# One decode-step kernel: the value loads of the paged attention move from GpSimd's queue to SyncE's, in one order with the key loads

## The chip, the cores and the metric

The kernel runs on one core of a Trainium2 chip. Its time is in device microseconds (us), the median of three runs. Engines have the profile's short names: PE is TensorE, DVE VectorE, ACT ScalarE, POOL GpSimd, SP SyncE. SP computes nothing here; it only issues DMAs and waits on semaphores.

## The reference, cut to what matters

One layer of a hybrid decoder, for a prompt of 256 tokens and for 8 decode batches of 4 tokens each. The stage that matters here is the decode attention, batch by batch:

```
k_all = concatenate([cache_fox_k[page_table], fk])       # 8 pages x 128 tokens, 6 heads x 128, then 4 new tokens
v_all = concatenate([cache_fox_v[page_table], fv])       # the same for the values
s = q k^T * HEAD_DIM**-0.5 + (c_q - c_k)                 # c: cumulative log-forget
fox_o = softmax(where(k_pos <= q_pos, s, -inf)) v_all
mem_o = softmax(q mk^T * HEAD_DIM**-0.5) mv              # 256 memory tokens, 4 heads x 128, own cache for each batch
```

Which pages a batch has stands in `page_table`, an input (8 pages for each of 8 batches), so the address of each page is read at run time. A page of keys or of values is 128 tokens x 768 floats, 393,216 bytes. The memory keys or values of a batch are 256 tokens x 512 floats, 524,288 bytes. After the attention come the output projection, a router and 32 experts, whose weights (three matrices of 2048 x 512 each) are read in whole.

## The kernel before, in words

Each engine has its own program, and semaphores set the order between them. The stages run one after another: norms and the input projection (up to some 450 us), the recurrence, head norms and outputs by token (to about 600 us), the attention of the prompt (to 655 us), the decode attention (655 to 819 us), the output projection (to about 970 us), the router and the experts.

**PE in the decode attention.** For each batch, `key_in(b, i)` transposes the keys in 14 units: units 0 to 11 read the eight key pages, two pages by three units, and units 12 and 13 the memory keys. Each unit waits for the pages that it reads (`k_in`, `mk_loaded`) and counts `kt_filled` when it is done, which frees pages. `decode_scores(b)` makes the scores, `max_row`, `max_spread` and `probs_in` stand between later key units, and `decode_values(b)` multiplies the probabilities by the value pages. It waits for the batch's eight value pages (`v_in`), for its memory values (`mv_loaded`), and at its end it counts `d_pv`. `decode_heads(b)` closes the batch. The order on PE is: keys of batch b + 1, values of b, scores of b + 1, heads of b, keys of b + 2, and so on.

**Buffers.** There is one set of eight key pages (`kpage`), reused by each batch as PE frees them, two sets of eight value pages (`vpage[par]`, par is the batch's parity), one buffer of memory keys (`mk_in`) and one of memory values (`mv_in`).

**Who loads what.** SP issues the key pages and the memory keys (lines 552 to 572). `load_key_page` first reads the page number from `ptab_row` in SBUF into a register (`value_load`, line 553), then waits for `kt_filled` (line 555), then issues the DMA (line 556). Six of batch 0's pages go ahead of the wait for the end of the prompt's attention (`pa_out`), since their buffers are free sooner. The loop over the other batches follows, then the first output-weight slice (line 576).

POOL issues the value pages and the memory values (lines 755 to 774): batch 0's pages as soon as it has finished its part of the recurrence and the projection is done, batch 0's memory values after `pa_out`, batch 1's pages after the outputs by token have been written, and then, for each batch, when `d_pv` says that the values of the batch before are used:

```
pool.wait_ge(d_pv, i * 2 + (u + 1))
load_mem_values(i * 2 + (u + 1))
load_values(i * 2 + (u + 2), u)
```

The two engines' DMAs go through two queues (in the profile q1, hardware_dynamic, for SP and q0, software_dynamic, for POOL) to the same 16 DMA engines. Nothing but the semaphores above orders the one queue against the other. After its last load POOL waits for the output projection and clears a strip of 32 rows.

Of the kernel before, what the change touches and what calls it, by code (L numbers as in the profile page):

```python
# [7 lines left out]
P = 128  # L8
KC = D // P
SEQ = 256  # L10
NB, NL = 8, 4
# [4 lines left out]
HF, HG, HM = 6, 6, 4  # L16
# [3 lines left out]
NPG, PG = 8, 128  # L20
POOL = 80
# [23 lines left out]
def build(nc, x_prompt, x_sample, cache_fox_k, cache_fox_v, cache_fox_logf, cache_mem_k, cache_mem_v,  # L45
# [7 lines left out]
    ds = bass.ds  # L53
# [16 lines left out]
    v_pages = cache_fox_v[0].rearrange("g t h d -> g t (h d)")  # L70

    ctx = ExitStack()
    with ctx:
        ctx.enter_context(nc.allow_non_contiguous_dma(reason="small vectors and column blocks"))

        def sb(name, shape, dt=f32):
            return ctx.enter_context(nc.sbuf_tensor(name, shape, dt))

        def sem(name):
            return ctx.enter_context(nc.semaphore(name))  # L80
# [30 lines left out]
        def view(off, *dims):  # L111
            n = 1
            for d in dims:
                n *= d
            a = arena[:, off:off + n]
            if len(dims) == 2:
                return a.rearrange("p (a b) -> p a b", b=dims[1])
            if len(dims) == 3:
                return a.rearrange("p (a b c) -> p a b c", b=dims[1], c=dims[2])
            return a  # L120
# [24 lines left out]
        def heads2(n):  # L145
# [22 lines left out]
        vpage = [[view(WORK + (4 + g) * FW, FW) for g in range(NPG)],  # L168
                 [view(MTOK + 5 * MEM + g * FW, FW) for g in range(6)] + [view(RAW + FV * T + g * FW, FW) for g in range(2)]]
# [4 lines left out]
        mv_in = view(MRAW + 2 * MW, 2, MW)  # L174
# [97 lines left out]
        ptab_row = sb("ptab_row", [1, NB * NPG], i32)  # L272
# [35 lines left out]
        blk_filled = sem("blk_filled")  # L308
# [23 lines left out]
        out_done = sem("out_done")  # L332
# [26 lines left out]
        h_again = sem("h_again")  # L359
# [21 lines left out]
        yt_filled = sem("yt_filled")  # L381
# [15 lines left out]
        s_loaded = [sem(f"s_loaded{n}") for n in range(2)]  # L397
# [18 lines left out]
        pa_out = sem("pa_out")  # L416
        ptrow_in = sem("ptrow_in")
# [3 lines left out]
        v_loaded = sem("v_loaded")  # L421
# [3 lines left out]
        q_clear = sem("q_clear")  # L425
        q_set = sem("q_set")
        d_scored = sem("d_scored")
        v_in, V_IN0 = (v_loaded, s_loaded[0]), (0, 16 * HG // 2)
        mv_loaded, MV0 = s_loaded[1], 16 * HG // 2
        d_row, d_row_min, d_spread = lb_diff, lb_exp, ssq_clear  # L430
        d_max = sem("d_max")
        d_exp = sem("d_exp")
# [5 lines left out]
        d_pv = sem("d_pv")  # L438
# [49 lines left out]
        NU = len(UNITS)  # L488
# [12 lines left out]
        def _(sp):  # L501
# [50 lines left out]
            def load_key_page(b, g, first=False):  # L552
                page = sp.value_load(ptab_row[0:1, ds(b * NPG + g, 1)], min_val=0, max_val=POOL - 1)
                if not first:
                    sp.wait_ge(kt_filled, b * KU + (3 * (g // 2) + 3 - KU))
                sp.dma_start(kpage[g], k_pages[ds(page, 1)].rearrange("g t n -> t (g n)")).then_inc(k_in[g], 16)

            def load_mem_keys(b, first=False):
                if not first:
                    sp.wait_ge(kt_filled, b * KU)  # L560
                sp.dma_start(mk_in, cache_mem_k[0][ds(b, 1)].rearrange("b (a t) h d -> t (b a) (h d)", t=P)).then_inc(mk_loaded, 16)
# [4 lines left out]
            for g in (3, 4):  # L566
                load_key_page(0, g, True)
            load_mem_keys(0, True)
            with sp.Fori(0, NB - 1) as i:
                for g in range(NPG):  # L570
                    load_key_page(i + 1, g)
                load_mem_keys(i + 1)


            sp.wait_ge(hn_done, NN)
# [91 lines left out]
        def _(pool):  # L667
# [80 lines left out]
            for n in range(2):  # L748
                pool.wait_ge(sts_out[n], 16 * HG // 2)


            pool.wait_ge(ptrow_in, 16)
            pool.wait_ge(blk_filled, 55)

            def load_values(b, par):
                for g in range(NPG):
                    page = pool.value_load(ptab_row[0:1, ds(b * NPG + g, 1)], min_val=0, max_val=POOL - 1)
                    pool.dma_start(vpage[par][g], v_pages[ds(page, 1)].rearrange("g t n -> t (g n)")).then_inc(v_in[par], 16)

            def load_mem_values(b):  # L760
                pool.dma_start(mv_in, cache_mem_v[0][ds(b, 1)].rearrange("b (a t) h d -> t (b a) (h d)", t=P)).then_inc(mv_loaded, 16)

            load_values(0, 0)
            pool.wait_ge(pa_out, NU)
            load_mem_values(0)
            pool.wait_ge(out_done, 16 * N_ROWS_OUT)
            load_values(1, 1)
            with pool.Fori(0, (NB - 2) // 2) as i:
                for u in range(2):
                    pool.wait_ge(d_pv, i * 2 + (u + 1))  # L770
                    load_mem_values(i * 2 + (u + 1))
                    load_values(i * 2 + (u + 2), u)
            pool.wait_ge(d_pv, NB - 1)
            load_mem_values(NB - 1)

            pool.wait_ge(wo_drained, KC)
            pool.memset(h_scaled[:, 2, :], 0.0).then_inc(consts_set, 1)
# [1311 lines left out]
N_ROWS_OUT = 8  # L2089
# [28 lines left out]
```

## Time and profile before

| | us |
|---|---|
| median of 3 runs (1952.29, 1952.88, 1958.1) | 1952.88 |
| the profiled execution | 1950.19 |
| its span, first to last instruction | 1948.6 |
| PE busy | 1571.3 (81%) |
| DVE busy | 435.0 (22%) |
| ACT busy | 223.2 (11%) |
| POOL busy | 77.4 (4%) |
| mean granted clock of PE | 0.881 |

How to read it: busy times are sums over the span, and matmuls are pipelined, so that a busy PE isn't PE at its peak. The granted clock is a share of 2.4 GHz: 1.00 is 2.4 GHz and 0.50 is 1.2 GHz. The waiting of SP and its DMA issues are in no engine's busy time; they are seen in the timeline of SP's queue, which the profile calls SPq (and POOL's POOLq).

### The profile page before, as it was taken

How to read it: one execution, taken by the hardware profiler on the slowest of the kernel's cores; microseconds unless marked ns; L12 is line 12 of the kernel's file. 1: busy time of each engine (PE TensorE's matmuls, PEld its weight loads, DVE VectorE, ACT ScalarE, POOL GpSimd, SP SyncE). 2: the span in 40 equal slices, each digit the busy share in tenths (PEclk: the TensorE clock that was granted, in tenths of full speed). 3: DMA queues.
4: the chain of work that ended last, by engine and by line, in shares of the span. 5: the costliest groups of instructions: out<-in, count | busy, mean ns of one | idle time of the engine just before them, and what ended most of it. 6: DMA issues, size and time to landing. Idle time of an engine off the chain costs nothing.

```text
span 1948.6 us, 24082 instructions
## 1 busy us (share of the span) xinstructions
PE 1571.3 (81%) x9517; PEld 925.7 (48%) x9517; DVE 435.0 (22%) x1138; ACT 223.2 (11%) x502; POOL 77.4 (4%) x141
## 2 busy tenths in 40 slices
PE   5999999999989899999967658677585766857656
PEld 4777777777746667677643213132141312313111
DVE  2200066645332434211220201102020020200201
ACT  3000101110042323111220000000000000000000
POOL 1000000012100122100000000000000000000000
PEclk9999999999986899899978888887788887878877
DMA  7434423234204599665369999999999999999996
GB/s 227 129 131 142 147 99 113 81 129 125 79 1 172 198 368 399 233 194 184 138 263 421 421 421 421 422 422 422 422 422 422 422 422 422 422 422 422 421 421 253
DMA packets 140424, 555.05 MB, mean 285 GB/s; under 512 B 16611, under 2 KB 71972, under 8 KB 90084
## 3 DMA queue, kind: packets, MB, share of 16 engines
q1 hardware_dynamic: 132084, 517.83, 67.0%
q0 software_dynamic: 8272, 36.25, 5.2%
q8 instruction: 50, 0.82, 0.2%
q14 instruction: 18, 0.15, 0.0%
HBM read 545.32 MB, written 8.72 MB: 284 GB/s over the span
## 4 chain that ended last, share of the span: by engine, by line
PE 57%; DMA 33%; DVE 3%; SPq 2%; ACT 2%; issue 2%; POOL 0%; DVEq 0%; ACTq 0%
PE PS L1544 19%; DMA arena<-in_w_up_e_dram 18%; DMA arena<-in_w_down_e_dram 9%; PE PS L1985 7%; PE PS L1932 7%; PE PS L2017 4%; DMA arena<-in_w_gate_e_dram 3%; PE PS L1964 3%; PE PS L2032 3%; PE PS L1804 2%; SPq L598 2%; DMA arena<-in_cache_mem_k_dram 2%; PE PS L1585 1%; PE PS L1864 1%; PE PS L1821 1%
## 5 line engine op out<-in xcount | busy, mean ns | idle before, releaser
L1985 PE MATMUL PS<-arena 128*32 128x512 f32 x2048 | 323.5, 779 | 225.6 <-DMA arena<-in_w_up_e_dram 148.1
L1544 PE MATMUL PS<-arena 128*128 128x288 f32 (+1 forms) x1728 | 434.2, 407 | 3.4 <-DVE arena L1036 1.1
L1544 PEld LDWEIGHTS PS<-arena 128*128 128x128 f32 x1728 | 328.4, 192 | 95.1 <-issue 12.9
L1985 PEld LDWEIGHTS PS<-arena 128*32 128x32 f32 x2048 | 78.6, 137 | 461.6 <-issue 188.6
L2017 PE MATMUL PS<-arena 128*32 128x512 f32 x1024 | 157.3, 776 | 73.6 <-DMA arena<-in_w_down_e_dram 73.6
L1932 PE MATMUL PS<-arena 128*128 128x288 f32 x512 | 129.5, 412 | 0.4 <-DVE arena L1308 0.4
L2017 PEld LDWEIGHTS PS<-arena 128*32 128x32 f32 x1024 | 37.8, 138 | 186.0 <-issue 98.0
L1461 DVE TENSOR_TENSOR arena<-arena,PS 128x512 f32<-128x512 f32 x8 | 5.5, 688 | 518.9 <-PE PS L1985 518.9
L1932 PEld LDWEIGHTS PS<-arena 128*128 128x128 f32 x512 | 97.2, 192 | 31.6 <-issue 5.5
L1964 PEld LDWEIGHTS PS<-arena 128*128 128x128 f32 x768 | 89.3, 196 | 9.7 <-issue 7.5
L1964 PE MATMUL PS<-arena 128*128 128x128 f32 x768 | 91.8, 281 | 2.0 <-ACT arena L965 2.0
L2032 PE MATMUL PS<-arena 128*128 128x512 f32 (+1 forms) x192 | 85.5, 598 | 0.0
L1471 DVE TENSOR_TENSOR arena<-arena,PS 128x512 f32<-128x512 f32 (+1 forms) x96 | 65.6, 684 | 18.8 <-PE PS L2032 18.8
L1804 PE MATMUL PS<-ident,arena 128*128 128x128 f32 x448 | 59.0, 288 | 9.1 <-DMA arena<-in_cache_fox_k_dram 5.4
L1466 DVE COPY arena<-PS 128x512 f32<-128x512 f32 x16 | 11.1, 692 | 221.1 <-PE PS L2017 221.1
L1804 PEld LDWEIGHTS PS<-ident,arena 128*128 128x128 f32 x448 | 53.4, 150 | 11.2 <-DMA arena<-in_cache_fox_k_dram 6.0
L2032 PEld LDWEIGHTS PS<-arena 128*128 128x128 f32 (+1 forms) x192 | 30.1, 163 | 55.7 <-issue 43.0
L980 ACT ACTIVATE arena<-PS 128x512 f32<-128x512 f32 x8 | 4.8, 597 | 372.0 <-PE PS L2004 372.0
L1272 DVE COPY arena<-PS 128x512 f32<-128x512 f32 x56 | 38.1, 688 | 28.7 <-PE PS L1804 28.6
L1107 DVE SCALAR_TENSOR_TENSOR arena<-arena 128x576 f32<-128x576 f32 x3 | 2.3, 759 | 187.2 <-ACT arena L814 187.2
L910 ACT ACTIVATE arena<-PS 128x512 f32<-128x512 f32 x56 | 33.4, 597 | 67.9 <-PE PS L1804 67.1
L1444 DVE TENSOR_TENSOR arena<-PS,g_ffn_r 128x512 f32<-128x512 f32 x32 | 22.1, 691 | 83.0 <-PE PS L1964 83.0
(335 smaller groups left out, 1190.4 us busy)
## 6 DMA issues: line engine op xcount, KB each, us to landing
arena<-in_w_gate_e_dram SPq DMA_DIRECT2D x128, 1024.0 KB, 17.6
arena<-in_w_up_e_dram SPq DMA_DIRECT2D x128, 1024.0 KB, 20.4
arena<-in_w_down_e_dram SPq DMA_DIRECT2D x128, 1024.0 KB, 18.5
arena<-in_w_in_dram SPq DMA_DIRECT2D x14, 3072.0 KB, 10.8
arena<-in_cache_fox_k_dram SPq DMA_DIRECT2D x64, 384.0 KB, 9.3
arena<-in_cache_fox_v_dram POOLq DMA_DIRECT2D x64, 384.0 KB, 7.5
arena<-in_w_out_dram SPq DMA_DIRECT2D x8, 2048.0 KB, 9.1
arena<-in_w_mem_kv_dram SPq DMA_DIRECT2D x2, 3072.0 KB, 17.9
```

Of the source, the lines that this page charges most:

```text
L598: sp.dma_start(unit[slot].rearrange("p (k n) -> p k n", n=src.shape[4]), src[ds(p * XQ + x, 1), g % 4].rearrange("e p k n -> p (e k) n")). ...
L910: act.activation(dst, PS[:, key_bank(b, i), :].rearrange("p (h t) -> p h t", h=dst.shape[1]), ACT.Copy).then_inc(kt_act, 1)
L1272: dve.tensor_copy(dst, PS[:, key_bank(b, i), :].rearrange("p (h t) -> p h t", h=dst.shape[1])).then_inc(kt_dve, 1)
L1444: dve.tensor_tensor(xgT[:, 4 * c:4 * c + 4, :], PS[:, 2 + c, :].rearrange("p (c s) -> p c s", s=P), g_ffn_r[:, 4 * c:4 * c + 4].rearrange( ...
L1471: dve.tensor_tensor(o, o, PS[0:w, 2 + n % 4, :], ALU.add).then_inc(part_added, 1)
L1544: last = pe.matmul(PS[0:m, bank, 0:w], wt[:, k, c:c + m], rhs[:, k, :], start=(k == 0), stop=(k == KC - 1))
L1804: last = pe.transpose(PS[:, key_bank(b, i), a * P:(a + 1) * P], src, ident[:, :])
L1932: last = pe.matmul(PS[:, n % 2, 0:T], wo_slot[(n // 2) % 3][:, k, c:c + P], cat[:, k, :], start=(k == 0), stop=(k == KC - 1))
L1964: last = pe.matmul(o, h_scaled[:, t, c * P:(c + 1) * P], pick_tok[:, t, :, :].rearrange("p x s -> p (x s)"), start=(t == 0), stop=(t == 2))
L1985: last = pe.matmul(PS[x * SLOTS:(x + 1) * SLOTS, which, :], xgT[:, kk, x * SLOTS:(x + 1) * SLOTS], wt[:, k, :], start=(kk == 0), stop=(kk ...
L2017: last = pe.matmul(PS[x * SLOTS:(x + 1) * SLOTS, YB[n], :], hT[:, q, x * SLOTS:(x + 1) * SLOTS], wt[:, n * 512:(n + 1) * 512], start=(q == ...
L2032: pe.matmul(PS[0:w, 2 + n % 4, :], gate_slot[:, t0:t0 + w], yslot[:, c * 512:(c + 1) * 512], start=True, stop=True).then_inc(part_filled, 1)
```

## The change: all four kinds of load in SP's program

The loads of values and memory values are taken out of POOL's program and put into SP's. The order on SP is now: key pages 3 and 4 and the memory keys of batch 0, value pages 0, memory values 0, keys 1, value pages 1, and then for each further batch its keys, the memory values of the batch before, and its value pages. The waits are the same (`out_done`, `d_pv`, `kt_filled`), each at the same load as before; the waits for `ptrow_in`, `blk_filled` and `pa_out` need not be repeated, since SP has passed its own. [...] The output-weight slice of line 576 comes after the last memory values.

```
-        v_in, V_IN0 = (v_loaded, s_loaded[0]), (0, 16 * HG // 2)
-        mv_loaded, MV0 = s_loaded[1], 16 * HG // 2
+        v_in, V_IN0 = (v_loaded, h_again), (0, 0)
+        mv_loaded, MV0 = yt_filled, 0
...
             load_mem_keys(0, True)
-            with sp.Fori(0, NB - 1) as i:
+            def load_values(b, par):
                 for g in range(NPG):
-                    load_key_page(i + 1, g)
-                load_mem_keys(i + 1)
+                    page = sp.value_load(ptab_row[0:1, ds(b * NPG + g, 1)], min_val=0, max_val=POOL - 1)
+                    sp.dma_start(vpage[par][g], v_pages[ds(page, 1)].rearrange("g t n -> t (g n)")).then_inc(v_in[par], 16)
+            def load_mem_values(b):
+                sp.dma_start(mv_in, cache_mem_v[0][ds(b, 1)].rearrange("b (a t) h d -> t (b a) (h d)", t=P)).then_inc(mv_loaded, 16)
+            def load_keys(b):
+                for g in range(NPG):
+                    load_key_page(b, g)
+                load_mem_keys(b)
+            load_values(0, 0)
+            load_mem_values(0)
+            sp.wait_ge(out_done, 16 * N_ROWS_OUT)
+            load_keys(1)
+            load_values(1, 1)
+            with sp.Fori(0, (NB - 2) // 2) as i:
+                for u in range(2):
+                    load_keys(i * 2 + (u + 2))
+                    sp.wait_ge(d_pv, i * 2 + (u + 1))
+                    load_mem_values(i * 2 + (u + 1))
+                    load_values(i * 2 + (u + 2), u)
+            sp.wait_ge(d_pv, NB - 1)
+            load_mem_values(NB - 1)
...
-            pool.wait_ge(ptrow_in, 16)
-            pool.wait_ge(blk_filled, 55)
-            def load_values(b, par):
-            ...
-            load_values(0, 0)
-            pool.wait_ge(pa_out, NU)
-            load_mem_values(0)
-            pool.wait_ge(out_done, 16 * N_ROWS_OUT)
-            load_values(1, 1)
-            ...
-            pool.wait_ge(d_pv, NB - 1)
-            load_mem_values(NB - 1)
```

## Rows read from the trace of the kernel before

**Rows 1.** The page's 40 slices of the span: busy tenths of the DMA engines.
```profile
DMA  7434423234204599665369999999999999999996
```

**Rows 2.** Windows: stretch, length, busy PE, PEld, DVE, ACT, POOL; clock, DMA share, GB/s.
```profile
610.00:615.00 5.00, 5.00 (x19) 4.08 (x19) 2.00 (x8) 1.58 (x6) 1.16 (x3) 0.50 1.03 407
...
810.00:815.00 5.00, 5.00 (x38) 1.36 (x32) 0.00 (x0) 0.00 (x0) 0.00 (x0) 0.50 0.00 0
...
656.00:776.00 120.00, 110.40 (x1312) 82.89 (x1311) 49.13 (x130) 40.84 (x84) 29.68 (x54) 0.96 1.00 380
...
1000.00:1940.00 940.00, 640.83 (x3998) 231.88 (x3987) 109.19 (x190) 30.50 (x47) 0.00 (x0) 0.82 1.00 415
```

**Rows 3.** Timeline of POOL: start, length, then the idle time before it and its releaser.
```profile
603.72 0.57 POOL L758 DMA_DIRECT2D arena<-in_cache_fox_v_dram  x1 [89.75 <-issue]
...
687.65 0.71 POOL L761 DMA_DIRECT2D arena<-in_cache_mem_v_dram  x1 [22.46 <-PE PS L1871]
...
705.21 0.71 POOL L761 DMA_DIRECT2D arena<-in_cache_mem_v_dram  x1 [6.23 <-PE PS L1871]
...
798.13 0.71 POOL L761 DMA_DIRECT2D arena<-in_cache_mem_v_dram  x1 [6.85 <-PE PS L1871]
```

**Rows 4.** The chain of waits in order of time, decode attention: start, length, what.
```profile
657.05 6.94 DMA arena<-in_cache_fox_k_dram
...
703.69 15.06 DMA arena<-in_cache_mem_k_dram
...
759.68 15.57 DMA arena<-in_cache_mem_k_dram
```

**Rows 5.** Waits of SP's queue, 650 to 822 us: total, times, longest.
```profile
SPq L556 <- PE PS L1804: 45.5, 8, 9.9
```

**Rows 6.** Timeline of SP's queue: first issue's start, time to the last one's end.
```profile
602.93 6.34 SPq L556 DMA_DIRECT2D arena<-in_cache_fox_k_dram  x6
...
655.95 1.44 SPq L556 DMA_DIRECT2D arena<-in_cache_fox_k_dram  x2
657.42 0.44 SPq L561 DMA_DIRECT2D arena<-in_cache_mem_k_dram  x1
...
694.73 8.78 SPq L556 DMA_DIRECT2D arena<-in_cache_fox_k_dram  x8
703.69 1.16 SPq L561 DMA_DIRECT2D arena<-in_cache_mem_k_dram  x1
...
777.25 0.38 SPq L561 DMA_DIRECT2D arena<-in_cache_mem_k_dram  x1
777.85 0.39 SPq L576 DMA_DIRECT2D arena<-in_w_out_dram  x1
```

**Rows 7.** Lines 553 and 556 on SP: nanoseconds min/median/max, first and last start.
```profile
L553 SPq TENSOR_LOAD <-ptab_row x64: 263/268/459, 602.0 to 776.0; - x64
...
L556 SPq DMA_DIRECT2D arena<-in_cache_fox_k_dram x64: 332/333/379, 602.9 to 776.7; - x64
...
DMA to landing us min/median/max: 3.1/9.3/12.9
```

**Rows 8.** Line 561 on SP, the memory keys, in the same form.
```profile
L561 SPq DMA_DIRECT2D arena<-in_cache_mem_k_dram x8: 383/383/1155, 657.4 to 777.3; - x8
...
DMA to landing us min/median/max: 5.1/13.2/16.4
```

**Rows 9.** Timeline of PE, the end of the stage, in the form of the timelines above.
```profile
775.30 1.09 PE L1804 MATMUL PS<-ident,arena 128*128 128x128 f32 x8 [1.94 <-DMA arena<-in_cache_mem_k_dram]
...
793.89 2.79 PE L1864 MATMUL PS<-arena 128*32 128x512 f32 x32
...
809.30 5.35 PE L1864 MATMUL PS<-arena 128*32 128x512 f32 x32 [0.70 <-DVE arena L1291]
...
819.26 3.12 PE L1932 MATMUL PS<-arena 128*128 128x288 f32 x6 [0.35 <-DVE arena L1308]
```

More of the change, by code:

```diff
@@ L749, in _ @@
                 pool.wait_ge(sts_out[n], 16 * HG // 2)
-            pool.wait_ge(ptrow_in, 16)
-            pool.wait_ge(blk_filled, 55)
-            def load_values(b, par):
[L756 to L761, printed above, removed]
-            load_values(0, 0)
-            pool.wait_ge(pa_out, NU)
-            load_mem_values(0)
-            pool.wait_ge(out_done, 16 * N_ROWS_OUT)
-            load_values(1, 1)
[L768 to L772, printed above, removed]
-            pool.wait_ge(d_pv, NB - 1)
-            load_mem_values(NB - 1)
             pool.wait_ge(wo_drained, KC)
```

## The prediction, made before the change was run

> **What bounds the kernel now.** I read the busy slices first: the DMA engines are at 9 tenths or more from the 22nd slice to all but the last, and before that only in slices 15 and 16, 682 to 779 us [rows 1]. Those two are the decode attention, the only stage that the diff touches. Its windows show three things: from 656 to 776 us TensorE is busy 110.4 of 120 us, the DMA share is 1.00 and 380 GB/s move [rows 2]; so PE and DMA are both close to their limit. Third I read the moments at which POOL issues a memory-value load, since each one marks the end of a batch's value matmuls: 687.65, 705.21 and so on to 798.13, six periods of 18.41 us on average, where an undisturbed one is 17.56 [rows 3]. The missing 0.85 us a batch is DMA: the chain of waits goes through key pages at 657.05 and through memory keys at 703.69 and 759.68 [rows 4]. Last I looked at the engine that is to take the extra work. SP waits 45.5 us in this stage for PE to free key pages, at most 9.9 at a time [rows 5]. That is all the room that it has.
>
> **What the change does, part by part.** Call the eight key pages of a batch K, its memory keys M, its value pages V, its memory values W. Before, SP issues K and M, POOL V and W. After, SP issues everything from one instruction stream, and V0, which POOL issues from 603.72 on [rows 3], comes only after SP's wait for the prompt attention at 655.
>
> *Price of a page.* SP's eight key pages at 694.73 take 8.78 us from the first issue's start to the last one's end [rows 6]. One issue is 0.33 us [rows 7], so they are (8.78 - 0.33)/7 = 1.207 us apart. Nothing holds them there: PE's transposes run well ahead by then, and the six ungated pages at 602.93 are (6.34 - 0.33)/5 = 1.202 apart [rows 6]. The rest of the 1.2 us is a serial chain ahead of each issue, the register load from the page table (268 ns [rows 7]) above all. A value page on SP in the loop has no row: its nearest are these, and the pair at 655.95, 1.44 - 0.33 = 1.11 apart [rows 6]. I take 1.20 for all and keep 1.11 as the low end for those that are not key pages of the loop. M comes 0.51 us after the last key page's issue (703.69 against 703.51 - 0.33), though its own issue once took 1.16 instead of 0.44 [rows 6]; I take 0.52 for each M and W, with 1.16 as the high end.
>
> *The sum on SP.* One batch is now 16 x 1.20 + 2 x 0.52 = 20.2 us of SP, more than the period of 18.41. SP has issued M0 by 657.42 + 0.44 = 657.9 [rows 6]. From there to the issue of M7 stand V0 to V6 and K1 to K7, 112 pages, and W0 to W5 and M1 to M6, 12 loads: 657.9 + 112 x 1.20 + 12 x 0.52 = 798.5. Before, M7 is issued at 777.25 [rows 6]. A second way: added are 56 pages and 6 loads, 70.3 us, of which SP's 45.5 us of waiting pay the larger part, 777.25 + 70.3 - 45.5 = 802; the 3.5 us between the two show how well the sum is known.
>
> *Do the waits on SP hold it up further?* The new wait for the end of the previous batch's values sits between M and W; behind it are queued W, V and the next K. It is passed at once: in this sum SP comes to it some 10 us after PE has passed that point. The same holds for the waits on freed key pages.
>
> *What that does to PE.* PE needs M7 for its last two transposes of batch 7. The landing of M took 5.1 us at least, 13.2 in the median, in the crowded queue [rows 8]. A batch is 16 pages of 393,216 B and two loads of 524,288 B, 7.34 MB. In 20.2 us that is 363 GB/s against the 407 of a full stretch [rows 2]; the queue drains, so I take 5.1: 803.6. The two transposes take 1.09 us and from the start of the value matmuls to POOL's next issue are 798.13 - 793.89 = 4.24 us [rows 3, 9]. So the values of batch 6 end at 808.9, against 798.13: **+10.8 us**. The other batches are late by less, 2 us more with each.
>
> *What is hidden.* V7 and W7 follow M7 on SP, until about 809.2; the value matmuls of batch 7 start 809.30 - 798.13 = 11.2 us after those of batch 6 end [rows 3, 9], at 820.1, so W7 has 10 us to land. At the median of 13.2 it would be some 2 us late. The first output-weight slice, now issued after W7 instead of at 777.85 [rows 6], is needed at 808.9 + (819.26 - 798.13) = 830; 2.1 MB at 407 GB/s are 5.2 us. POOL's freed time is worth nothing here: nobody on the path waits for it. V0's bytes go from a stretch with room into this one, and fit while SP is the slower.
>
> *After the stage.* Output projection and experts start from its end; the weight ring loads at a share of 1.00 and 415 GB/s up to the end [rows 2] and starts when the projection lets it. So the delay passes through whole.
>
> The profiled execution took 1950.19 us, its span 1948.6: 1950.19 + 10.8 = 1961.0. It lies 2.7 under the median of 1952.88, from which the sum is 1963.7. I forecast 1962.5, between them.
>
> *Two rules weighed.* A page costs SP 1.20 us to issue and the engines 393,216 B / 407 GB/s = 0.97 us to move [rows 2, 6]. The Trainium skill ("DMA: Bandwidth & Descriptors", "Issuing engines are not separate DMA queues") says that issuing from several engines only saves the sequencer's time to initiate a DMA, "usually small relative to the DMA itself". The trace disagrees with the "usually": the register load makes it larger here. By the rule the outcome is rival A. The same page ("Latency and other measured facts") gives the register load a floor of about 600 ns; the trace has 268 and decides. An estimate by that page would be 1.53 us a page and another 37 us.
>
> **Rivals.**
> A. *SP's issue doesn't bound, the transfers do.* Then until M7 114 pages and 14 memory loads pass from 658 on: 114 x 0.97 + 14 x 1.29 = 128.6, M7 has landed near 788.7 with 2 us of latency, and batch 6 ends at 794. PE's own 17.56 us a batch say 6 x 17.56 after 684 to 687, 789 to 793. So -4 us, about 1946 to 1949: no difference. For it: share 1.00 now. Against it: the 1.207 us between ungated issues.
> B. *The other side: one ordered queue ends the stalls.* Place: pages 3 and 4 of batch 0, which now share the engines with W0 and V1; the chain has 6.94 us there [rows 4], of which 3.1 are the least landing of a key page [rows 7], so 3.8 go; and each batch falls to 17.56, 6 x 0.85 = 5.1. Price -8.9, 1941 to 1944. It decides where a page issue is under (17.56 - 1.04)/16 = 1.03 us. Against it: no page on SP shows less than 1.11.
> C. *PE's clock.* PE now idles over 2 us a batch. The value matmuls at a granted clock of 0.50 (the lower level, 1.2 GHz) took 5.35 us, at full clock 2.79 [rows 2, 9]. PE becomes the bound once 17.56 us of work become 20.2, so when the lower level holds over a quarter of the stage. At half of it, 17.56/0.76 = 23.1 a batch: 6 x 4.7 = +28, 1979. Against it: 0.96 with the present stalls [rows 2].
>
> **How the numbers follow.** Forecast 0.80, A 0.09, B 0.04, C 0.07. The forecast's own ends: the 64 pages outside the loop's keys at 1.11 take 5.8 off, a landing of 3.1 another 2.0, giving +3; memory loads at 1.16 add 7.7 and a landing of 13.2 adds 8.1, giving +26, but both at once need a full queue. Its middle is +6 to +18. The range 1955.5 to 1973 holds most of this middle and of its two ends; outside lie A, B and most of C. This kernel can't tell less than 0.3% (5.9 us) from no change. Of the forecast's 0.80 some 0.06 stay under that: slower 0.74 + 0.07 = 0.81, same 0.15, faster 0.04.
>
> **What would show it.** Right: SP's key pages and value pages 1.2 us apart without a break, its wait for PE gone from 45.5 us to nearly none, M7 issued near 798, periods of 20 us, some 360 GB/s, PE waiting for key pages and memory keys in every batch. Wrong: SP still waiting for PE, pages less than 1.05 us apart, or a period that follows the clock.

## The result and the profile after

The changed kernel takes 1964.07 us (median of 15 runs, 1958.24 to 1965.93) against 1952.88 for the kernel before: a ratio of 1.0047 with a 95% interval of 1.0035 to 1.0059, so 6.8 to 11.5 us slower. The forecast was 1962.5, and slower.

The profiled execution took 1965.0 us, its span 1963.2, 14.6 more than before. Four marks on PE divide that up: the first key transposes of the decode stage, the last value matmuls of the first and of the seventh batch, and the first output projection. Timeline of PE in the kernel after: start, length, then the idle time before it and its releaser.

```profile
657.03 1.97 PE L1803 MATMUL PS<-ident,arena 128*128 128x128 f32 x16 [0.37 <-ACT arena L903]
...
689.01 0.65 PE L1870 MATMUL PS<-arena 128*32 128x128 f32 x16
...
805.15 1.09 PE L1803 MATMUL PS<-ident,arena 128*128 128x128 f32 x8 [0.81 <-DMA arena<-in_cache_mem_k_dram]
806.70 2.79 PE L1863 MATMUL PS<-arena 128*32 128x512 f32 x32 [0.46 <-DMA arena<-in_cache_mem_v_dram]
...
809.96 0.64 PE L1870 MATMUL PS<-arena 128*32 128x128 f32 x16
...
822.47 4.88 PE L1863 MATMUL PS<-arena 128*32 128x512 f32 x32 [0.70 <-DVE arena L1290]
...
832.48 4.21 PE L1931 MATMUL PS<-arena 128*128 128x288 f32 x8 [0.36 <-DVE arena L1307]
```

The same marks before, of which the last is in [rows 9]:

```profile
655.27 1.97 PE L1804 MATMUL PS<-ident,arena 128*128 128x128 f32 x16 [0.37 <-ACT arena L904]
...
686.31 0.65 PE L1871 MATMUL PS<-arena 128*32 128x128 f32 x16
...
797.15 0.64 PE L1871 MATMUL PS<-arena 128*32 128x128 f32 x16
```

The stage starts 1.8 us later, ahead of anything that the change touches (in the profiles taken here it starts between 653.4 and 658.1). From its start to the seventh batch's values it takes 152.9 us in place of 141.9: 0.9 of the 11.0 us are lost up to the first batch's values and 10.1 in the six periods after them, which are 20.16 us in place of 18.47. From there to the projection 0.4 more, and after it 1.4. So the loss is in the periods, and SP's queue shows what sets them (start of the first issue, time to the end of the last, as in [rows 6]):

```profile
659.19 0.44 SPq L561 DMA_DIRECT2D arena<-in_cache_mem_k_dram  x1
660.37 7.97 SPq L573 DMA_DIRECT2D arena<-in_cache_fox_v_dram  x8
668.39 0.44 SPq L576 DMA_DIRECT2D arena<-in_cache_mem_v_dram  x1
669.59 7.98 SPq L556 DMA_DIRECT2D arena<-in_cache_fox_k_dram  x8
...
708.57 8.77 SPq L556 DMA_DIRECT2D arena<-in_cache_fox_k_dram  x8
717.52 0.38 SPq L561 DMA_DIRECT2D arena<-in_cache_mem_k_dram  x1
718.00 0.41 SPq L576 DMA_DIRECT2D arena<-in_cache_mem_v_dram  x1
719.17 8.37 SPq L573 DMA_DIRECT2D arena<-in_cache_fox_v_dram  x8
728.95 8.99 SPq L556 DMA_DIRECT2D arena<-in_cache_fox_k_dram  x8
...
798.34 0.38 SPq L561 DMA_DIRECT2D arena<-in_cache_mem_k_dram  x1
798.83 0.41 SPq L576 DMA_DIRECT2D arena<-in_cache_mem_v_dram  x1
800.00 8.11 SPq L573 DMA_DIRECT2D arena<-in_cache_fox_v_dram  x8
810.67 0.39 SPq L576 DMA_DIRECT2D arena<-in_cache_mem_v_dram  x1
811.12 0.46 SPq L599 DMA_DIRECT2D arena<-in_w_out_dram  x1
```

SP issues without a break: one run of pages ends where the next one's register load begins. Its waits from 640 to 840 us (total, times, longest) say the same:

```profile
SPq L553 <- ACT arena L903: 46.6, 1, 46.6
SPq L601 <- PE PS L1879: 20.6, 1, 20.6
SPq L576 <- PE PS L1870: 2.4, 1, 2.4
```

The 45.5 us that SP waited for freed key pages [rows 5] are gone from the list; what is left lies before the stage, after it, and at the very last memory values. PE now waits for transfers in small pieces, and the DMA engines carry less. PE's waits for DMA in the stage, and the window that answers to [rows 2] (same columns):

```profile
PE PS L1803 <- DMA arena<-in_cache_fox_k_dram: 8.7, 13, 2.2
...
PE PS L1803 <- DMA arena<-in_cache_mem_k_dram: 2.7, 5, 1.0
PE PS L1863 <- DMA arena<-in_cache_mem_v_dram: 2.5, 6, 0.5
```
```profile
656.00:776.00 120.00, 107.36 (x1256) 76.42 (x1256) 44.30 (x119) 36.45 (x74) 0.00 (x0) 0.97 0.98 357
```

Before, the same list has two waits for key pages, 5.4 us, and two for memory keys, 3.4, so it has grown by 5.1 us, half of what is lost. The other half isn't in this list. PE's weight loads, which overlap its matmuls, wait 13.7 us for key pages in place of 6.0.

Nothing here says by itself that SP is at fault: the DMA share is still 0.98, and a reader could call the stage bound by transfers. What tells them apart is the time to landing. In the table of DMA issues (line, count, size, median us to landing) it has fallen by nearly half for key pages, from the 9.3 of [rows 7] to 5.1, and from 13.2 [rows 8] to 6.4 for memory keys:

```profile
arena<-in_cache_fox_k_dram SPq DMA_DIRECT2D x64, 384.0 KB, 5.1
...
arena<-in_cache_mem_k_dram SPq DMA_DIRECT2D x8, 512.0 KB, 6.4
```

Each transfer is quick because few stand before it, and PE waits all the same: the issuer is late, not the engines. So far that is a reading of one profile; the experiments test it.

### The profile page after: what moved, and what is told of

Read it like the earlier page. It is cut to its first block, busy times and chain, and to the rows that moved or that the text cites. A ratio compares the mean times of both kernels' runs of the same rounds, so it can differ in the third digit from the quotient of the medians.

```text
span 1963.2 us, 23999 instructions
## 1 busy us (share of the span) xinstructions
PE 1587.0 (81%) x9517; PEld 927.5 (47%) x9517; DVE 435.8 (22%) x1138; ACT 223.0 (11%) x502; POOL 37.0 (2%) x68
## 4 chain that ended last, share of the span: by engine, by line
PE 51%; DMA 35%; SPq 5%; DVE 3%; issue 3%; ACT 2%; POOL 0%; DVEq 0%; ACTq 0%
PE PS L1543 19%; DMA arena<-in_w_up_e_dram 18%; DMA arena<-in_w_down_e_dram 9%; PE PS L1984 7%; PE PS L1931 7%; DMA arena<-in_w_gate_e_dram 6%; PE PS L2016 3%; PE PS L1963 2%; SPq L621 2%; PE PS L2031 2%; PE PS L1584 1%; SPq L572 1%; PE PS L1719 1%; SPq L573 1%; SPq L553 1%
## 5 line engine op out<-in xcount | busy, mean ns | idle before, releaser
L1984 PE MATMUL PS<-arena 128*32 128x512 f32 x2048 | 336.1, 805 | 216.6 <-DMA arena<-in_w_up_e_dram 139.7
L2016 PE MATMUL PS<-arena 128*32 128x512 f32 x1024 | 151.2, 749 | 76.3 <-DMA arena<-in_w_down_e_dram 76.3
L1803 PE MATMUL PS<-ident,arena 128*128 128x128 f32 x448 | 64.2, 292 | 11.9 <-DMA arena<-in_cache_fox_k_dram 8.7
L1803 PEld LDWEIGHTS PS<-ident,arena 128*128 128x128 f32 x448 | 53.2, 150 | 19.2 <-DMA arena<-in_cache_fox_k_dram 13.7
L1271 DVE COPY arena<-PS 128x512 f32<-128x512 f32 x56 | 38.4, 688 | 30.1 <-PE PS L1803 29.6
```

Of the source, the lines that this page charges most:

```text
L1271: dve.tensor_copy(dst, PS[:, key_bank(b, i), :].rearrange("p (h t) -> p h t", h=dst.shape[1])).then_inc(kt_dve, 1)
L1803: last = pe.transpose(PS[:, key_bank(b, i), a * P:(a + 1) * P], src, ident[:, :])
L1984: last = pe.matmul(PS[x * SLOTS:(x + 1) * SLOTS, which, :], xgT[:, kk, x * SLOTS:(x + 1) * SLOTS], wt[:, k, :], start=(kk == 0), stop=(kk ...
L2016: last = pe.matmul(PS[x * SLOTS:(x + 1) * SLOTS, YB[n], :], hT[:, q, x * SLOTS:(x + 1) * SLOTS], wt[:, n * 512:(n + 1) * 512], start=(q == ...
```

## The experiments

Two theories (theory B isn't rival B of the prediction). I: SP's instruction stream is the bound, some 1.2 us for each page whose number it reads from the table. B: the stage loses because batch 0's value pages (V0, 3.1 MB) now pass in a crowded stretch and because one queue carries less than two. All times below are compared with runs of the kernel before on the same chip.

**1. Value pages without the table.**

```
-   page = sp.value_load(ptab_row[0:1, ds(b * NPG + g, 1)], min_val=0, max_val=POOL - 1)
-   sp.dma_start(vpage[par][g], v_pages[ds(page, 1)]...
+   sp.dma_start(vpage[par][g], v_pages[ds(b * NPG + g, 1)]...
```

> The changed kernel, but the value pages are read at fixed places (page b x 8 + g of the pool) without the page table, so that SP needs no register load for them; this leaves out the lookup for the values. All bytes, queues and orders stay. Theory I (SP's issue rate is the bound): a value page costs SP about 0.5 us in place of 1.15, so a batch falls from 20.1 us of SP to 8 x 1.21 + 8 x 0.5 + 1 = 14.7, under PE's 17.56; the stage is again held by PE and the transfers, last memory keys issued before 785, whole kernel within 4 us of the kernel before (1948 to 1955). Theory B (the moved bytes of the first value pages and one queue in place of two make the loss): nothing of that is changed, so 1960 to 1966 as in the changed kernel.

Measured: 1951.43 us, a ratio of 0.9996 (0.9975 to 1.0018) to the kernel before. The loss is gone with V0 late and with one queue, as theory I has it. The last memory keys are issued at 783.23, as expected. As many bytes in the same order cost some 9 us or nothing, by the work that SP does ahead of each value page.

**2. Only V0 late, on POOL.**

```
-   load_values(0, 0)
    pool.wait_ge(pa_out, NU)
+   load_values(0, 0)
```

> The kernel before, with one part of the change: POOL issues batch 0's value pages after the wait for the prompt attention and not before it, so 3.1 MB more pass in the decode stage; two queues as before. Theory I: SP keeps its waiting time, so only the bytes count; 3.1 MB are 7.7 us of transfers at 407 GB/s, a part of which fits into the 685 to 700 us stretch that moved only some 310 GB/s: +2 to +6 us on the kernel before. Theory B (the bytes of V0 are the whole loss): +9 to +12 us, as in the changed kernel.

Measured: 1960.0 us, ratio 1.0048 (1.0031 to 1.0065), 6 to 13 us slower. My estimate of +2 to +6 fails, and theory B is right for this kernel. PE's marks show where it happens: 40.6 us from the start of the stage to the first batch's values (31.0 before), then six periods of 18.45, as before. It is all lost in the first batch:

```profile
675.63 0.65 PE L1804 MATMUL PS<-ident,arena 128*128 128x128 f32 x4 [0.89 <-DMA arena<-in_cache_fox_k_dram]
...
678.16 0.66 PE L1804 MATMUL PS<-ident,arena 128*128 128x128 f32 x4 [0.98 <-DMA arena<-in_cache_fox_k_dram]
...
681.05 1.97 PE L1804 MATMUL PS<-ident,arena 128*128 128x128 f32 x8 [2.23 <-DMA arena<-in_cache_fox_k_dram]
...
693.95 0.64 PE L1871 MATMUL PS<-arena 128*32 128x128 f32 x16
```

POOL issues 17 loads in a row there, and K1, which PE needs first, shares the engines with all of them: SP has issued the last page of K1 by 668.0, but it takes 18.8 us to land, twice the median before of 9.3 [rows 7].

**3. Only V0 early, the rest on SP.**

```
-   load_values(0, 0)                      # SP, after pa_out
+   for g in range(NPG): ...               # POOL, early, as before
```

> The changed kernel, with one part undone: batch 0's value pages are issued by POOL early, as in the kernel before (on a semaphore of their own); all else stays on SP. Theory I: eight pages of 1.1 us less in SP's chain, so the last memory keys are issued 8.7 us earlier and the kernel is 8 to 9 us faster than the changed one, +0 to +4 us on the kernel before; SP is still the bound, with periods of 20 us. Theory B: the same 8 us, but with periods back under 19 us.

Measured: 1952.35 us, ratio 1.0012 (0.9989 to 1.0036): against the changed kernel some 7 us come back by the ratios and 10.6 by the medians, where both theories said 8 to 9. The periods decide. Late in the stage they are still 20 us, so SP is still the bound, and the gain is eight issues less ahead of it:

```profile
758.49 0.65 PE L1877 MATMUL PS<-arena 128*32 128x128 f32 x16
...
778.48 0.64 PE L1877 MATMUL PS<-arena 128*32 128x128 f32 x16
...
798.40 0.64 PE L1877 MATMUL PS<-arena 128*32 128x128 f32 x16
```

The first batch's values come 27.8 us after the start of the stage, 3.3 earlier than in the kernel before, and the slower periods give that back.

**4. The table read twice.**

```
+   sp.value_load(ptab_row[0:1, ds(b * NPG + g, 1)], min_val=0, max_val=POOL - 1)
    page = sp.value_load(ptab_row[0:1, ds(b * NPG + g, 1)], min_val=0, max_val=POOL - 1)
```

> The changed kernel, but SP reads the page number of each value page from the table twice. The second read is one more register load with what follows it, about 0.55 us (0.27 load, 0.15 and 0.02 register work, gaps). Theory I: 56 value pages stand before the last memory keys, so these are issued 56 x 0.55 = 31 us later and the kernel takes about 31 us more than the changed one, 1990 to 1998. Theory B: transfers are the same, and SP's queue has slack, so less than 5 us more, under 1970.

Measured: 1991.65 us, ratio 1.0207 (1.0168 to 1.0246). The last memory keys are issued at 828.05, from a first issue of memory keys at 658.76:

```profile
828.05 0.38 SPq L561 DMA_DIRECT2D arena<-in_cache_mem_k_dram  x1
830.26 11.84 SPq L574 DMA_DIRECT2D arena<-in_cache_fox_v_dram  x8
```

That is 169.3 us of SP in place of 139.2 (798.34 - 659.19), 30.1 more or 0.54 a page, and the kernel follows it almost one to one: 31 us by the ratios.

**5. The table read once for both pages.** Keys and values of a batch lie at the same page numbers, and V follows K on SP, so the eight numbers can stay in registers.

```
     load_key_page: ... sp.dma_start(kpage[g], ...)
+                       pages[g] = page
-   page = sp.value_load(...)
-   sp.dma_start(vpage[par][g], v_pages[ds(page, 1)]...
+   sp.dma_start(vpage[par][g], v_pages[ds(pages[g], 1)]...
```

> The changed kernel, but SP keeps the eight page numbers that it read for a batch's keys in registers and issues the value pages of that batch with them: same bytes, same order, same results, one table read for two pages. Theory I (SP's issue rate): as with the value pages read without the table, 14.7 us of SP a batch, periods of 18.4 us set by the transfers, 1949 to 1955, no difference to the kernel before. Theory B (one queue and the late first value pages): 1960 to 1966, as in the changed kernel; that the run without the table was fast would then lie in its places being in order in memory.

Measured: 1951.91 us, ratio 0.9986 (0.9967 to 1.0005). As in experiment 1, so it wasn't the order in memory. In the shortest run of eight, 4.84 us, a value page from a register comes some 0.6 us after the one before it, so keys (1.21) and values come to some 0.9 in the mean. The periods are (800.62 - 689.76)/6 = 18.48 us. The window and the landings show the other kind of bound: the engines carry 381 GB/s, as before the change (380), and landing takes twice as long as in the changed kernel, since each transfer has more of others ahead of it.

```profile
676.61 4.84 SPq L575 DMA_DIRECT2D arena<-in_cache_fox_v_dram  x8
...
710.94 6.95 SPq L575 DMA_DIRECT2D arena<-in_cache_fox_v_dram  x8
```
```profile
689.76 0.65 PE L1872 MATMUL PS<-arena 128*32 128x128 f32 x16
...
800.62 0.65 PE L1872 MATMUL PS<-arena 128*32 128x128 f32 x16
```

```profile
656.00:776.00 120.00, 113.34 (x1308) 85.34 (x1309) 48.73 (x131) 40.38 (x83) 0.00 (x0) 0.94 1.00 381
```
```profile
arena<-in_cache_fox_k_dram SPq DMA_DIRECT2D x64, 384.0 KB, 10.5
```

SP doesn't rest here, though the expectation gave it only 14.7 us of work a batch. From the memory keys at 709.94 to those at 784.07, four batches, it takes 18.5 us a batch with hardly a gap, and its list of waits shows none for PE until the last memory values. The later runs of eight value pages last 6.6 to 7.9 us. What is longer is the issue instruction itself, 0.67 us in the median (0.65 in experiment 1) where it was 0.33 in the changed kernel. Issues of values in the changed kernel and here (nanoseconds min/median/max):

```profile
L573 SPq DMA_DIRECT2D arena<-in_cache_fox_v_dram x64: 332/333/726, 660.4 to 807.8; - x64
```
```profile
L575 SPq DMA_DIRECT2D arena<-in_cache_fox_v_dram x64: 374/670/1872, 660.8 to 792.6; - x64
```

What holds these instructions no run shows directly. That they are long where landings are long, and short where landings are short, fits that the queue takes an issue only as fast as the transfers before it move on: SP would then be held by the transfers and not the other way round.

**6. Read once, and V0 early on SP.**

```
+   for g in (3, 4):
+       pages[g] = sp.value_load(ptab_row[0:1, ds(g, 1)], min_val=0, max_val=POOL - 1)
+   sp.wait_ge(blk_filled, 55)
+   for g in range(NPG): sp.dma_start(vpage[0][g], v_pages[ds(pages[g], 1)]...
    sp.wait_ge(pa_out, NU)
    ...                                   # key pages 3 and 4 from the registers, memory keys
-   load_values(0, 0)
```

> The same with batch 0's value pages issued by SP ahead of its wait for the prompt attention, so that all eight table reads and V0's bytes leave the decode stage. Theory I: SP isn't the bound (14.7 us a batch) and the stage carries 3.1 MB less, so it starts as early as with V0 early on POOL (first batch's values some 3 us earlier than before) and goes on at 17.6 to 18.4 us a batch: 3 to 8 us faster than the kernel before, 1944 to 1949. Theory B: one queue carries less than two, so 1952 or more.

Measured: 1941.87 us (1939.72 to 1944.69), ratio 0.9939 (0.9916 to 0.9962): 7 to 16 us faster than the kernel before, more than I expected, and the fastest of all. A part of the difference is clock: five of its six runs had a mean granted clock of 0.888 to 0.893, and their median is 1940.7; the twelve of 29 runs of the kernel before with 0.884 or more have a median of 1949.9, which makes it 9.2 us. In its trace the first batch's values come 25.0 us after the start of the stage (31.0 before) and the periods are 18.30 (18.47), 7.0 us in all; with the last batch and the way to the projection it is 8.7. Those last 1.7 us go at least in part with the clock at the last value matmuls, which take 4.14 us here and 5.35 before; experiments 2, 3, 7 and 8 have them too.

```profile
658.05 1.97 PE L1809 MATMUL PS<-ident,arena 128*128 128x128 f32 x16 [0.37 <-ACT arena L909]
...
661.23 1.09 PE L1809 MATMUL PS<-ident,arena 128*128 128x128 f32 x8 [1.21 <-DMA arena<-in_cache_fox_k_dram]
...
662.66 4.03 PE L1809 MATMUL PS<-ident,arena 128*128 128x128 f32 x32 [0.34 <-DMA arena<-in_cache_fox_k_dram]
...
683.09 0.64 PE L1876 MATMUL PS<-arena 128*32 128x128 f32 x16
...
792.89 0.64 PE L1876 MATMUL PS<-arena 128*32 128x128 f32 x16
```

The one queue and the table reads done ahead were not tried apart here. Experiment 3, which has the order but not the cheap issues, gains 3.3 of these 6.0 us in the first batch.

**7. Two queues, the key pages first.**

```
    pool.wait_ge(pa_out, NU)
+   for g in (3, 4): pool.wait_ge(k_in[g], 32)
    load_mem_values(0)
```

> The kernel before, but POOL waits with batch 0's memory values and batch 1's value pages until key pages 3 and 4 of batch 0 have landed. It tries rival B's first part, that the two queues' sharing costs PE at the start. Theory I: PE's 3.8 and 1.6 us of waiting there fall by 2 to 3 us together, and part of it comes back as the later loads land later: -3 to 0 us on the kernel before. Against it: the transfers are the bound from there on, so 0 to +2.

Measured: 1955.95 us, ratio 1.0012 (0.9998 to 1.0027): no gain. PE's waits for pages 3 and 4 fall from 3.8 and 1.6 us to 1.61 and 0.65, but four waits for K1 come in their place, 4.0 us together, and the first batch's values come 34.0 us after the start in place of 31.0. Holding one queue back moves the collision; it doesn't order the two.

**8. The extra read where there is room.**

```
    # the kernel before, in load_key_page
+   sp.value_load(ptab_row[0:1, ds(b * NPG + g, 1)], min_val=0, max_val=POOL - 1)
    page = sp.value_load(ptab_row[0:1, ds(b * NPG + g, 1)], min_val=0, max_val=POOL - 1)
```

> The kernel before, but SP reads the page number of each key page from the table twice, the same extra work for each page as in the run with the table read twice (0.6 us a page, 4.8 us a batch). There SP waits some 6.5 us a batch, so theory I says that the slack takes it: 0 to +4 us on the kernel before, against some +30 for the same reads in the changed kernel. If an extra read costs in itself, wherever it stands, +25 to +34.

Measured: 1954.52 us, ratio 1.001 (0.9989 to 1.0031). The same extra work for as many pages, which costs 31 us in the changed kernel, is at most 6 us here and not told from nothing; SP's wait for freed pages pays most of it, 17.2 us where it was 45.5 [rows 5]:

```profile
SPq L557 <- PE PS L1805: 17.2, 6, 6.2
```

## Why the prediction was right

**The price of a page.** Forecast 1.20 us on SP. Key pages in the loop are (8.77 - 0.33)/7 = 1.21 apart, value pages in the loop (8.37 - 0.33)/7 = 1.15, both in straight code (7.97 - 0.33)/7 = 1.09. So the low end of 1.11 was the right one for the straight code, and 1.20 some 5% too much for the rest of the value pages.

**The sum on SP.** Forecast 140.6 us from the end of the first memory keys' issue to the last memory keys' (657.9 to 798.5). Measured 138.7 (659.63 to 798.34). The second way, which came to 802, was the worse one.

**The waits.** The new wait for `d_pv` was said to be passed at once. It is: its only wait is 2.4 us, ahead of the last memory values, after the last key page.

**From M7 to the values.** Here 5.1 us for the landing was too little: PE's transposes start 6.8 us after the issue. And the memory values of batch 6, issued right behind M7, land after it, 0.46 us that I hadn't counted. These errors and the shorter chain on SP nearly cancel. W7 is issued 12.5 us later than before (810.67 against 798.13 [rows 3]), 10.8 without the 1.8 that the stage starts later; the forecast was 10.8. That the sum hit so closely is in part luck of the signs.

**What was called hidden.** V7 and W7 are issued by 811 and their matmuls start at 822.47 on PE's and DVE's account; the first weight slice, issued at 811.12, was needed at 832.48. No run shows a gain from POOL's free time.

**Rivals.** A (transfers bound, not SP) is false for the changed kernel and true for experiment 5: with the issue made cheap, the stage goes at the transfers' pace and the time is that of before. B named a real place: the waits for pages 3 and 4 fall from 5.4 us to 1.75 + 1.22 = 3.0 in the changed kernel, but SP had V0's issues in front of K1, so PE waited 2.20 + 0.20 us for K1's first pages, and the first batch's values were no earlier. PE's waits for pages 3 and 4, before and in the changed kernel:

```profile
661.05 1.41 PE L1804 MATMUL PS<-ident,arena 128*128 128x128 f32 x8 [3.82 <-DMA arena<-in_cache_fox_k_dram]
664.04 5.87 PE L1804 MATMUL PS<-ident,arena 128*128 128x128 f32 x32 [1.57 <-DMA arena<-in_cache_fox_k_dram]
```
```profile
660.75 1.09 PE L1803 MATMUL PS<-ident,arena 128*128 128x128 f32 x8 [1.75 <-DMA arena<-in_cache_fox_k_dram]
663.06 5.28 PE L1803 MATMUL PS<-ident,arena 128*128 128x128 f32 x32 [1.22 <-DMA arena<-in_cache_fox_k_dram]
```

In experiment 6, where the issues that nothing holds come to some 0.9 us in the mean of keys and values, under B's point of 1.03, the gain is there, but by another split than B's: 6.0 us in the first batch (B had 3.8) and 1.0 in the six periods (B had 5.1), which stay at 18.3 us and don't fall to 17.56. C (the clock) didn't occur: 0.97 in the stage.

**Where the undoing misleads.** Experiments 2 and 3 alone would have given V0's bytes the whole blame: late, they cost 8 us; early, the loss is gone. Both are true, by different mechanisms: on POOL V0 delays K1 at the engines, on SP it stands in front of K1 as eight issues. Only making the issue cheap with the bytes left in place (1, 5) told them apart.

The Trainium skill's rule that the time to initiate a DMA is usually small beside the DMA itself ("DMA: Bandwidth & Descriptors", "Issuing engines are not separate DMA queues") doesn't hold in the changed kernel, where an issue with its table read is 1.15 to 1.21 us against 0.97 us of transfer (393,216 B at the 407 GB/s of [rows 2]). With the table read shared, the mean is some 0.9 where nothing holds the issues, still not small, but under the transfer, and the batch falls from 20.16 to 18.48 us.

## What to carry to other kernels

Before issues are moved to one engine, add up that engine's instruction stream for one period, register loads and address work included, and set it against the period: an idle engine in the profile may have only its waiting time to give. One ordered queue was worth having here, where two queues collide, but only with an issuer that stays ahead of the transfers; short landings together with a waiting consumer showed that it didn't. An issuer without a pause isn't the bound by that alone: see whether its instructions are work of its own (table reads, addresses) or issues that have grown long. Where addresses come from a table, read each entry once and keep it in a register.

## What the runs showed that I had not expected

Two queues that share the engines can cost more than the bytes: 3.1 MB are 7.7 us at 407 GB/s, and in these profiles they cost 9.5 us at the first batch on POOL's queue. With SP's ordered queue and cheap issues the first batch is only 0.6 later than before (31.66 us from the start of the stage to the first batch's values in experiment 5, 31.04 before). With V0 early in both, SP's ordered queue with cheap issues gains 6.0 us at the first batch (experiment 6 against the kernel before); leaving V0's bytes out of that queue gains 6.6 (experiment 6 against 5). So the order was worth about as much as the bytes, and the changed kernel hid that gain behind SP's issue rate.
